# Decoder trunk on one core: the second layer on 256 real tokens in two blocks instead of 272 in three

## What is computed

```python
h = jnp.concatenate([meta_tokens, x], axis=1)                      # 16 + 256 tokens
# layer 0: recurrence, dense mixer (all 272 tokens)
k_nope, k_rope, v = shared_latent_kv(h, ...)                       # all 272 tokens
mix = mla_block(rms_norm(h, b_pre_norm), k_nope, k_rope, v, ...)   # softmax over keys <= query
h = h + rms_norm(mix, b_post_norm)
ff = moe_swiglu(rms_norm(h, m_pre_norm), ...)                      # top 2 of 8 experts per token
h = h + rms_norm(ff, m_post_norm)
return h[:, N_META:]
```

## Time and profile before

| | |
|---|---|
| median of 3 runs | 1722.38 us (1721.02 to 1723.44) |
| profiled execution, first to last instruction | 1719.5 us |
| PE busy | 1609.4 us (94%) |
| DVE busy | 1254.0 us (73%) |
| ACT busy | 1049.4 us (61%) |
| POOL busy | 18.2 us (1%) |
| mean granted TensorE clock | 0.952 of full |
| read from memory | 423 MB |
| rounding L1056, remainder L1417 (128 x 2048), mean of 338 each | 1.914 and 2.287 us |
| DVE L1453, an operation of 128 x 24 in the routing | 0.18 us |
| ACT L869, squares of the residual, eight, 592.1 to 597.0 | one in 0.70 us |
| ACT L856, copy of a 64 x 272 output | 0.39 us |
| chain that ended last | PE 83%, DVE 10%, ACT 4% |

### The profile page before, as it was taken

One profiled execution on the slowest core, in us unless ns is written; L12 is line 12 of the kernel. 1 busy time (PEld: TensorE's weight loads), 2 busy tenths in 40 slices (PEclk: granted clock), 3 DMA queues, 4 the chain that ended last, 5 costly groups with the idle time before them and its releaser, 6 DMA issues.

```text
span 1719.5 us, 22645 instructions
## 1 busy us (share of the span) xinstructions
PE 1609.4 (94%) x8288; PEld 1332.7 (78%) x8288; DVE 1254.0 (73%) x1367; ACT 1049.4 (61%) x1141; POOL 18.2 (1%) x15
## 2 busy tenths in 40 slices
PE   6877999997799959999999999999999999999996
PEld 5877999996655847787787787787787787787784
DVE  5975545437565357878878878888888888888887
ACT  4764444434555336667666767667667667767665
POOL 0000000000000110000000000000000000000000
PEclk9988999999887859999999999999999999999998
DMA  8335455541211118999999999999999999999992
GB/s 251 120 101 172 147 173 179 175 132 59 91 39 61 62 49 292 329 333 340 340 320 339 342 322 339 339 325 341 336 320 345 334 334 335 336 337 324 331 343 100
DMA packets 222195, 425.02 MB, mean 247 GB/s; under 512 B 7728, under 2 KB 76464, under 8 KB 222144
## 3 DMA queue, kind: packets, MB, share of 16 engines
q1 hardware_dynamic: 221968, 423.80, 71.7%
q0 software_dynamic: 176, 0.53, 0.1%
HBM read 423.25 MB, written 1.05 MB: 247 GB/s over the span
## 4 chain that ended last, share of the span: by engine, by line
PE 83%; DVE 10%; ACT 4%; issue 2%; DMA 1%; SPq 0%; DVEq 0%; POOL 0%; ACTq 0%
PE bank L374 24%; PE bank L376 23%; PE bank L375 23%; PE bank L621 3%; PE bank L395 2%; DVE w_lo L1171 2%; PE bank L602 2%; PE bank L656 1%; PE bank L538 1%; DVE w_lo L1417 1%; DVE x_lo L1509 1%; ACT w_hi L1056 1%; ACT w_hi L849 1%; DVE xc L1250 1%; PE bank L519 1%
## 5 line engine op out<-in xcount | busy, mean ns | idle before, releaser
L1417 DVE TENSOR_TENSOR w_lo<-raw,w_hi 128x2048 fp32r<-128x2048 f32 x338 | 766.7, 2287 | 174.8 <-ACT w_hi L1056 173.8
L1056 ACT CAST w_hi<-raw 128x2048 fp32r<-128x2048 f32 x338 | 644.9, 1914 | 312.9 <-PE bank L376 312.9
L374 PE MATMUL bank<-w_hi,x_hi 128*128 128x512 f32 x896 | 378.5, 422 | 4.8 <-DVE x_lo L1509 4.8
L375 PE MATMUL bank<-w_lo,x_hi 128*128 128x512 f32 x896 | 354.6, 396 | 0.0
L376 PE MATMUL bank<-w_hi,x_lo 128*128 128x512 f32 x896 | 354.3, 395 | 0.0
L1171 DVE TENSOR_TENSOR w_lo<-raw,w_hi 128x2048 fp32r<-128x2048 f32 (+7 forms) x91 | 152.6, 1698 | 150.1 <-ACT w_hi L849 150.0
L374 PE MATMUL bank<-u_hi,w_hi 128*128 128x272 f32 (+1 forms) x632 | 188.8, 299 | 26.3 <-DVE u_lo L1198 14.3
L374 PEld LDWEIGHTS bank<-w_hi,x_hi 128*128 128x128 f32 x896 | 168.9, 189 | 55.8 <-issue 16.5
L375 PEld LDWEIGHTS bank<-w_lo,x_hi 128*128 128x128 f32 x896 | 168.9, 188 | 47.9 <-issue 11.5
L376 PEld LDWEIGHTS bank<-w_hi,x_lo 128*128 128x128 f32 x896 | 168.7, 188 | 41.3
L376 PE MATMUL bank<-u_hi,w_lo 128*128 128x272 f32 (+1 forms) x632 | 186.0, 294 | 0.0
(11 more groups left out here) (258 smaller groups left out, 1772.6 us busy)
## 6 DMA issues: line engine op xcount, KB each, us to landing
raw<-in_m_w_gate_up SPq DMA_DIRECT2D x226, 1024.0 KB, 6.9
raw<-in_m_w_down SPq DMA_DIRECT2D x112, 1024.0 KB, 7.1
raw<-in_f_w_gate_up SPq DMA_DIRECT2D x24, 1024.0 KB, 5.2
raw<-in_f_w_down SPq DMA_DIRECT2D x12, 1024.0 KB, 5.1
raw<-in_a_w_in SPq DMA_DIRECT2D x10, 1024.0 KB, 9.9
raw<-in_a_w_out SPq DMA_DIRECT2D x8, 640.0 KB, 4.5
raw<-in_b_w_o SPq DMA_DIRECT2D x4, 1024.0 KB, 5.5
raw<-in_b_w_uq SPq DMA_DIRECT2D x4, 576.0 KB, 4.1
```

Source lines behind the costliest of these rows:

```text
L374: nc.tensor.matmul(o, a[0], b[0], start=start, stop=False)
L375: nc.tensor.matmul(o, a[0], b[1], start=False, stop=False)
L1056: nc.scalar.copy(w_hi[(NC0 + c) % SPLIT][:], raw[slot][:]).then_inc(hi_done, 1)
L1417: nc.vector.tensor_tensor(w_lo[s][:], raw[(NC0 + c) % RAW][:], w_hi[s][:].bitcast(F32), ALU.subtract)\
```

## The change

The second layer from the queries on works on the 256 real tokens only, columns 16 to 272, in two blocks of 128 (`TB`, `NB` = 2); the first layer, keys and values stay on 272.

- Matmuls of 272 columns for the latent of the queries, the queries and `b_out` have 256, and so have the element operations on them (`at=REAL`).
- A head's scores lie in one bank: block 0 against the 16 meta keys and block 0 (144 columns), block 1 against 288 columns of which 16 are a copy of the meta keys, masked. Keys are stored in that layout (`KX` = 288), the two masks in one tile `s_mask` that GpSimd builds. The maximum comes out scaled and negated, without the operation of L1388.
- A head's probabilities are turned in four transposes of 128 x 128, one of which carries the meta keys of both blocks; values of the meta tokens lie in a zeroed tile `v_meta`. The weighting has four matmuls of 256, 128, 128 and 128 columns. An even head writes partitions 0 to 63 and an odd one 64 to 127 of the same bank (6 or 7), and rounding and remainder read the pair from there.
- Router, gather, gates, scatter, final norm and stores go over two blocks. There are four scatters per pass, after chunks 2, 6, 10 and 14, and four last ones.
- GpSimd gets a memset of 128 x 2048, the mask, and the copies of the rotated keys in three pieces and of the meta keys in two; the zero fills of `h_thi` and `h_tlo` go.

```diff
-TB = [(0, 128), (128, 128), (256, 16)]
+XB = [(0, 128), (128, 128), (256, 16)]
+TB = [(META, 128), (META + 128, 128)]
+NB = len(TB)
+KB = [(0, META)] + TB
+KX = META + P + META + P
+SW = 448
+ALL, REAL = slice(0, T), slice(META, T)
...
-SCATTER = (2, 6, 10, 14, 18, 22)
+WIDE = {"cq": REAL, "bo": REAL}
+
+SCATTER = (2, 6, 10, 14)
...
+            s_mask = sb("s_mask", [P, SW], stack=ph)
+
+        s_sb = mix.rearrange("p k n -> p (k n)")[:, 0:3 * SW].rearrange("p (h n) -> p h n", h=3)
...
-        SC = [(0, 128), (128, 256), (384, T)]
+        SC = [(0, META, META + P), (META + P + 16, 0, KX)]
...
-                    last = product(ps[0:width, 0:T], [x[:, k, c0:c0 + width] for x in wc],
-                                   [x[:, k, 0:T] for x in act], k == 0, k == kn - 1)
+                    last = product(ps[0:width, at], [x[:, k, c0:c0 + width] for x in wc],
+                                   [x[:, k, at] for x in act], k == 0, k == kn - 1)
...
+            def scores(h):
+
+                ps = bank_of("s", h)
+                for b in range(NB):
+                    c, k0, kn = SC[b]
+                    last = nc.tensor.matmul(ps[:, c:c + kn], qT[h // 4 % 2][:, h % 4, P * b:P * b + P], kT[:, h, k0:k0 + kn],
+                                            start=True, stop=True)
+                mark(last, ("tile", TN[("s", h)]))
+
             def turn_probs(h):
 
                 pe.wait_ge(prob_done, h + 1)
                 ps = bank_of("pt", h)
                 p = s_sb[:, h % 3, :]
-                for b, (t0, n) in enumerate(TB):
-                    for kb in range(b + 1):
-                        c, kn = SC[b][0] + P * kb, TB[kb][1]
-                        o = (0, 144, 160)[kb] + t0
-                        last = nc.tensor.transpose(ps[0:kn, o:o + n], p[0:n, c:c + kn], ident[0:n, 0:n])
+                for i, c in enumerate((0, SC[1][0] + META, SC[1][0] + META + P + META, P)):
+                    last = nc.tensor.transpose(ps[:, P * i:P * i + P], p[:, c:c + P], ident)
                 mark(last, ("tile", TN[("pt", h)]))
 
             def weigh(h):
 
-                ps = bank_of("o", h)
+                ps = banks[6 + h // 2 % 2]
+                if h % 2 == 0 and h >= 4:
+                    pe.wait_ge(act_lo, PART["o"] + h // 2 - 1)
                 pe.wait_ge(emptied["A"], EMPTIED[TN[("pt", h)]])
-                for kb, (t0, kn) in enumerate(TB):
-                    o = (0, 144, 160)[kb] + t0
-                    last = nc.tensor.matmul(ps[0:VD, t0:T], v_tok[0:kn, kb, VD * h:VD * h + VD], pT[0:kn, h % 2, o:o + T - t0],
-                                            start=(kb == 0), stop=(kb == 2))
-                mark(last, ("tile", TN[("o", h)]))
+                o, p, c = ps[VD * (h % 2):VD * (h % 2) + VD, :], pT[:, h % 2, :], slice(VD * h, VD * h + VD)
+                nc.tensor.matmul(o[:, 0:2 * P], v_tok[:, 0, c], p[:, 0:2 * P], start=True, stop=False)
+                nc.tensor.matmul(o[:, P:2 * P], v_tok[:, 1, c], p[:, 2 * P:3 * P], start=False, stop=False)
+                for b in range(NB):
+                    last = nc.tensor.matmul(o[:, P * b:P * b + P], v_meta[:, b, c], p[:, 3 * P:4 * P], start=False,
+                                            stop=(b == 1))
+                mark(last, ("weighed", h))
...
-                    pe.wait_ge(krope_copied, 1)
-                for b, (t0, n) in enumerate(TB):
-                    ps = bank_of("s", (h, b))
-                    mark(nc.tensor.matmul(ps[0:n, 0:SC[b][1]], qT[g % 2][:, h % 4, t0:t0 + n], kT[:, h, 0:SC[b][1]],
-                                          start=True, stop=True), ("tile", TN[("s", (h, b))]))
+                    pe.wait_ge(krope_copied, 3)
+                scores(h)
...
                 for part, src in enumerate((h_thi, h_tlo)):
-                    for b in range(3):
+                    for b in range(NB):
                         last = nc.tensor.matmul(banks[half][:, :], sel[:, b, :], src[:, b, NT * half:NT * half + NT],
-                                                start=(part == 0 and b == 0), stop=(part == 1 and b == 2))
+                                                start=(part == 0 and b == 0), stop=(part == 1 and b == NB - 1))
...
-                                    pe.wait_ge(added, it * 6 + (i - 1))
-                                emark(scatter(banks[(7, 4, 5)[i % 3]], i % 3, i // 3), ("scattered", i))
+                                    pe.wait_ge(added, it * 4 + (i - 1))
+                                emark(scatter(banks[(7, 4, 5)[i % 3]], i % NB, i // NB), ("scattered", i))
...
-            for i in range(6):
-                mark(scatter(banks[(7, 6, 5, 4, 3, 2)[i]], i // 2, i % 2), ("last_scattered", i))
+            for i in range(2 * NB):
+                mark(scatter(banks[(7, 6, 5, 4)[i]], i // 2, i % 2), ("last_scattered", i))
...
+            pool.wait_ge(pads_zeroed, 1)
+            stair = cn("mask0")[:, META:META + P]
+            nc.gpsimd.memset(v_meta[:], 0.0)
+            nc.gpsimd.memset(s_mask[:], 0.0).then_inc(pool_step, 1)
+            pool.wait_ge(pool_step, 1)
+            nc.gpsimd.tensor_copy(s_mask[:, 0:P], stair)
+            nc.gpsimd.tensor_copy(s_mask[:, SW - P:SW], stair)
+            nc.gpsimd.memset(s_mask[:, SW - P - META:SW - P], -1.0e30).then_inc(mask_done, 1)
+
+            pool.wait_ge(mask_done, 1)
             pool.wait_ge(krope_done, 1)
             at(pool, "tile", TN[("cq", KQ - 1)])
-            nc.gpsimd.tensor_copy(kT[NOPE:QK, :, :], rope_a[NOPE:QK, None, :].to_broadcast([ROPE, HEADS, T]))\
-                .then_inc(krope_copied, 1)
+            r = rope_a[NOPE:QK, None, :].to_broadcast([ROPE, HEADS, T])
+            nc.gpsimd.tensor_copy(kT[NOPE:QK, :, 0:META + P], r[:, :, 0:META + P])
+            nc.gpsimd.tensor_copy(kT[NOPE:QK, :, META + P:KX - P], r[:, :, 0:META])
+            nc.gpsimd.tensor_copy(kT[NOPE:QK, :, KX - P:KX], r[:, :, META + P:T]).then_inc(krope_copied, 1)
+            for half in range(2):
+                pool.wait_ge(krope_copied, half + 1)
+                pool.wait_ge(emptied["A"], EMPTIED[TN[("kn", 4 * half + 3)]])
+                k = kT[0:NOPE, 8 * half:8 * half + 8, :]
+                nc.gpsimd.tensor_copy(k[:, :, META + P:KX - P], k[:, :, 0:META]).then_inc(krope_copied, 1)
 
             pool.wait_ge(res_done, RES["bo"] + 1)
...
+                nc.scalar.copy(v_meta[0:META, 0, c], ps[0:META, :])
+                nc.scalar.copy(v_meta[32:32 + META, 1, c], ps[0:META, :]).then_inc(emptied["A"], 1)
+                for b in range(NB):
+                    empty("v", (b + 1, half), v_tok[:, b, c])
...
-                    empty("o", t, sq[r:r + VD, t // 2, :], rows=slice(0, VD))
-                if h >= LAG + 3 and h % 2:
-                    k = (h - LAG - 3) // 2
-                    act.wait_ge(emptied["A"], EMPTIED[TN[("o", 2 * k + 1)]])
-                    nc.scalar.copy(u_hi[:, k, :], sq[:, k, :]).then_inc(act_hi, 1)
+                        at(act, "weighed", t - 2)
+                    nc.scalar.copy(pT[:, t % 2, :], ps[:, :]).then_inc(emptied["A"], 1)
+                if LAG + 1 < h <= HEADS + LAG and h % 2 == LAG % 2:
+                    k = (h - LAG - 2) // 2
+                    at(act, "weighed", 2 * k + 1)
+                    nc.scalar.copy(u_hi[:, k, REAL], banks[6 + k % 2][:, 0:SEQ]).then_inc(act_hi, 1)
...
+                    ps = at_tile(dve, "s", h)
+                    for b in range(NB):
+                        c, _, kn = SC[b]
+                        last = nc.vector.tensor_tensor_reduce(s_sb[:, h % 3, c:c + kn], ps[:, c:c + kn], s_mask[:, c:c + kn],
+                                                              -(QK ** -0.5), 3.0e38, ALU.add, ALU.min,
+                                                              nbias[:, i + b:i + b + 1])
+                    last.then_inc(emptied["V"], 1)
...
+            for i in range(2 * NB):
                 at_last(dve, rounds, i)
                 y = y_acc[:, i // 2, NT * (i % 2):NT * (i % 2) + NT]
-                nc.vector.tensor_tensor(y, y, banks[(7, 6, 5, 4, 3, 2)[i]][:, :], ALU.add).then_inc(added, 1)
-            dve.wait_ge(fin_sum, 6)
```

332 lines of the change are left out of this document (159 added, 173 removed).

## The result

The change takes 1643.28 us (median of 4 runs, 1642.96 to 1645.83) against 1722.38; the ratio is 0.9545, with the 95% interval from 0.9533 to 0.9556. It is faster by 79 us. The profiled execution has a span of 1641.4 us, 78.1 less than before.

A forecast was written before the change was run, and what follows sets the result against it. TensorE was taken to bound the expert loop and the attention. Eight terms summing to 51.3 us, taken off 1722.4, gave 1671 us; the range was 1652 to 1688.

The forecast's parts named there:

- Expert loop: Eight expert passes: fewer scatters, gather products, norms, gates and a transpose save 3.15 us per pass, 25.2 us in all.
- Attention: Second-layer attention: 3.6 us from cheaper heads in sixteen and 2.0 from fewer TensorE gaps, together 5.6 us.
- Rival A: Attention: the clock stays high there, giving 1650 us, or 1660 for half of it; chance 0.20.
- The price of a head: TensorE in the attention: a head goes from 3.2 to 2.96 us high and from 5.7 to 5.45 low.
- The gaps: Attention: with less ScalarE and VectorE work per head, part of TensorE's 6.5 us of gaps goes, 2.0 us.
- Router and routing: Before the expert loop: router loses a third of each of eight feature blocks, 7.3 us; routing saves 5.5 us.
- Columns, −2.7 and element operations, −0.5: 408 matmuls lose 16 columns and 48 key matmuls gain 16, saving 2.7 us; element operations on 256 columns save 0.5.
- GpSimd: Rotated-key copy in three pieces lets VectorE's remainders in between: 1.0 us saved, between 2.5 and −0.5.
- End: After the loop: two last scatters and a block's scaling and addition go, the last store grows: 3.5 us saved.
- Rival C: Expert loop: loads become the bound; 1696 us if 335 GB/s were the most, 1684 for half; chance 0.09.
- B: Attention: the clock falls where it was high; 1706 us at worst, 1688 for the likely half; chance 0.12.
- D: Expert loop: colliding loads lower the carried rate below 326 GB/s, making the change slower than before; chance 0.02.

The follow-up runs named there:

- before_wide: The kernel before with 128 queries instead of 16 as the stationary side of each head's third score matmul, same columns streamed: 1712.89 us, ratio 0.9944.
- after_tiny: The change with four more weighting matmuls of 16 columns in each head: 1647.33 us.
- after_body32: The change with 32 unused bytes ahead of hT that only layer one and attention feel: 1641.41 us.
- after_keys_late3: The change with 32 bytes ahead of hT in the first phases and GpSimd's rotated-key copies held until VectorE has the first queries' chunk's remainder: 1633.95 us.

## Why the prediction was wrong, and where it was right

- *Expert loop, −25.2.* The steps were right: with 32 bytes put in, which bring a matmul back to 0.233 us, the loop's passes last 128.5 us (forecast 128.7) and the stage gains 25.2 for 23.7. What failed is the unspoken step ahead of them, that a matmul of 128x512 keeps its 0.233 us. It is 0.2272 to 0.228 with the new places, 15.6 us in the loop. The diff said nothing of speed, but it did reorder the tiles.
- *Attention, −5.6: the step that failed in the prediction's own terms.* It charged the low clock's price for as long as before, 48 us by the mean of 0.74; by the mean of 0.93 over 70 us some 10 were left. Rival A, the clock stays high, was what came; I gave it 0.20 because of the gapless low stretch, and took that as evidence against it. `before_wide` shows that the stretch spoke of the narrow matmuls in it. I weighed the rule of the Trainium skill (TensorE: Matmul & The Clock Gate, Part 1), that activity releases the throttle, with gaps alone in mind; no row before had wide matmuls at that place, so the row could not refute it. A's time, 1650 to 1660, was also the nearest. An estimate of the clock's worth by the prices of the earlier trace rows: 38 us fewer at 3.2 for 5.7 are 17 us.
- *The price of a head.* Fitted from the earlier trace rows as 1.61 ns a column and 0.12 us a matmul, it gave 2.96 us high; measured are 2.60. The fit laid on every matmul what the kernel before paid, at least in part, for its narrow ones: with its third score matmul widened its scores fall from 1.42 to 1.22 us, and a narrow one has a least time of 0.11 us (`after_tiny`). Without it, weighting takes 1.23 instead of 1.52, scores 0.84 instead of 0.94. A head gains 0.6 and not 0.24, 10 us in sixteen instead of 3.8 (the sum had 3.6).
- *The gaps, −2.0 of the attention's 5.6.* They went the other way: TensorE's gaps grew from 6.5 to 11 us. It now waits 5.9 us for VectorE's probabilities (L1436) and 4.5 us for ScalarE's copies of them (L1075), where it waited 3.9 (L1399) and 1.8 (L1036). The three together, 17 by the clock and 10 by the heads less 4.4 by the gaps, come to 22.6; measured are 22.8. The split is an estimate.
- *Router and routing.* A block takes 2.02 us, not 1.8:

```profile
582.82 1.00 PE L597 MATMUL bank<-gw,hT 128*128 128x8 f32 x4
...
584.84 1.00 PE L597 MATMUL bank<-gw,hT 128*128 128x8 f32 x4
```

  so a block gains 0.71 us and not 0.91: the third block had been the cheaper one. From the first to the last start of the eight it is 13.35 us for 17.82 (the first two run partly at the full clock), with the last block 5.2 us for the 7.3. The rest to the gather is 4.3 us, forecast 3.2. GpSimd still meets one VectorE operation of the chain (L1485, 1.83 us).
- *Columns, −2.7 and element operations, −0.5.* At the start they do not show. Layer one's new addresses cost 2.4 us; but without them (`after_body32`) the first scores start at 465.2 us, no earlier than before, and of what took the forecast 1.5 us only 0.2 is traced, the stretched remainders. In the output product TensorE is busy 28.6 us instead of 30.2, at the same mean clock (0.94); but it waits 2.3 us for the last pair's remainder (L1444, at 540.2), where it waited 0.6 (L1407).
- *GpSimd, −1.0.* Wrong: VectorE's four remainders took 6.29 us after 6.11. By the rule of the Trainium skill (SBUF — State Buffer, Who interferes with whom) the term was 0, and that was right. I had put the hope above it that VectorE gets in between three pieces. The 3.8 us that the copies cost VectorE can be had by placing them later: the stretch takes 10.1 us in `after_keys_late3` and 13.9 in the change.
- *End, −3.5.* Right: last SiLU to end gains 5.5 where the rest of the loop and the end were 5.0, and 5.0 with the 32 bytes.
- *Rival C, loads.* Refuted: 350 GB/s over a pass, all its loads within 8.7 us, ScalarE waits for TensorE. *B and D* did not come. 335 GB/s was no ceiling.

## What to carry to other kernels

Narrow work at an edge (16 rows of a third block) cost three times here: its own least time (0.11 us for 16 columns), a price at the change between wide and narrow (0.2 us in a head's scores), and the clock of the wide work around it. When a change removes such work, price the clock as well. A price per matmul that is fitted to a mix of wide and narrow ones does not hold for wide ones alone. A gapless stretch at the low clock is not evidence that the clock can't rise with other matmuls in the same place. When tiles are added, removed or reordered, compare the start-to-start distance of a matmul that the change leaves alone, at the same granted clock: here it was what gave the placement away.

## What the hardware showed that was not expected

TensorE's pace depends on where both operands of a matmul start: 0.2269 us for 512 columns with equal offsets modulo 256 bytes, 0.232 to 0.235 at most of the other offsets tried, with the core's other engines idle, and 0.2272 against 0.2335 us in the loop, 15.6 us of this kernel. Why is not shown. For 272 columns the best offset was another (stationary 64 beyond: 0.1231 against 0.125). The granted clock was back after some 3 us in the change, with wide matmuls, where it had stayed low for 17 us with narrow ones and no gap. And a stationary operand of 16 columns among wide ones cost 0.2 us in a head's scores at the full clock, with the same columns streamed (1.42 against 1.22 us).
